# Hybrid trunk step on one core: head order, D's decay and first conv, diagonal taps, norm sums, final store

## The reference

```python
h = rmsnorm(x, norm_pre)
p = split_cols(h @ w_in)
oa = s5_branch(...); ob = hgrn2_branch(...); oc = gla_branch(...)
od = rglru_branch(...)                  # width-4 conv, then RG-LRU; decay = -8 * r * softplus(-lam)
oe = mem_attend(p["e_q"], mk, mv)       # 4 heads over 256 memory tokens, mk, mv from rmsnorm(mem)
pb = einsum("ntcw,cwd->ntcd", branches * silu(gates), w_branch)
merged = einsum("ntcd,ntcd->ntd", sigmoid(h @ w_merge), pb)
x = x + rmsnorm(merged @ w_out, norm_post)
```

## Time and profile before

| | |
|---|---|
| median of 3 runs | 2093.11 us (2087.61 to 2093.49) |
| the profiled execution's own time | 2093.22 us |
| its span, first to last instruction | 2091.4 us |
| TensorE busy | 1990.5 us (95%) |
| DVE, ACT, POOL busy | 61%, 43%, 20% |
| mean granted TensorE clock | 0.974 |

### The profile page before, as it was taken

One profiled execution on the slowest core, in us unless ns is written; L12 is line 12 of the kernel. 1 busy time (PEld: TensorE's weight loads), 2 busy tenths in 40 slices (PEclk: granted clock), 3 DMA queues, 4 the chain that ended last, 5 costly groups with the idle time before them and its releaser, 6 DMA issues.

```text
span 2091.4 us, 36635 instructions
## 1 busy us (share of the span) xinstructions
PE 1990.5 (95%) x15254; PEld 1906.4 (91%) x15254; DVE 1278.6 (61%) x2092; ACT 906.3 (43%) x1307; POOL 411.4 (20%) x708
## 2 busy tenths in 40 slices
PE   6999986999999999999999999999999999999995
PEld 5889986999998989898999999999999999999994
DVE  6654437777665656565777777777565565554543
ACT  4533433444553434343555555545333333433342
POOL 3678877875000000000000000000100000000000
PEclk9999998999998989898999999999999999999997
DMA  6766754555443434444444444444655444555441
GB/s 237 256 245 243 264 181 134 174 182 187 157 159 134 160 136 151 145 149 159 139 143 153 141 150 144 147 140 137 219 165 191 161 155 149 193 178 165 151 162 66
DMA packets 91222, 350.46 MB, mean 168 GB/s; under 512 B 11728, under 2 KB 11872, under 8 KB 87472
## 3 DMA queue, kind: packets, MB, share of 16 engines
q1 hardware_dynamic: 76032, 278.17, 40.3%
q0 software_dynamic: 12144, 49.85, 6.7%
q10 hardware_dynamic: 2880, 20.09, 2.5%
HBM read 321.15 MB, written 26.92 MB: 166 GB/s over the span
## 4 chain that ended last, share of the span: by engine, by line
PE 58%; DVE 7%; ACT 4%; issue 3%; DMA 0%; POOL 0%; ACTq 0%; DVEq 0%
PE ps L1581 57%; DVE w_lo L1034 2%; DVE g_X L1028 1%; DVE g_X L1034 1%; ACT g_t L566 1%; ACT w_hi L566 1%; ACT L566 1%; DVE g_X L1037 0%; ACT g_X L566 0%; DMA a_h<-in_a_h 0%; DVE g_b L1439 0%; PE ps L1869 0%; DVE acc L1031 0%; DVE acc L1028 0%; DVE g_k L1034 0%
## 5 line engine op out<-in xcount | busy, mean ns | idle before, releaser
L1581 PE MATMUL ps<-h_hi,w_hi 128*128 128x288 f32 x2960 | 892.9, 302 | 39.6 <-DVE w_lo L1034 22.9
L1034 DVE TENSOR_TENSOR w_lo<-raw,w_hi 128x1024 fp32r<-128x1024 f32 x522 | 649.6, 1255 | 439.5 <-ACT w_hi L566 436.0
L1581 PE MATMUL ps<-h_hi,w_lo 128*128 128x288 f32 x2960 | 877.8, 297 | 0.0
L1581 PE MATMUL ps<-h_lo,w_hi 128*128 128x288 f32 x2960 | 875.4, 296 | 0.0
L566 ACT ACTIVATE w_hi<-raw 128x1024 fp32r<-128x1024 f32 x522 | 547.3, 1056 | 655.3 <-PE ps L1581 646.9
L1581 PEld LDWEIGHTS ps<-h_hi,w_hi 128*128 128x128 f32 x2960 | 559.7, 189 | 60.6 <-issue 43.0
L1581 PEld LDWEIGHTS ps<-h_hi,w_lo 128*128 128x128 f32 x2960 | 560.7, 189 | 2.3 <-issue 1.9
L1581 PEld LDWEIGHTS ps<-h_lo,w_hi 128*128 128x128 f32 x2960 | 561.7, 190 | 0.0
L1581 PE MATMUL ps<-br_hi,w_hi 128*128 128x288 f32 x640 | 196.0, 306 | 0.5 <-DVE d_gate L1040 0.5
L1581 PE MATMUL ps<-br_hi,w_lo 128*128 128x288 f32 x640 | 192.9, 301 | 0.0
L1581 PE MATMUL ps<-br_lo,w_hi 128*128 128x288 f32 x640 | 192.6, 301 | 0.0
(11 more groups left out here) (369 smaller groups left out, 2465.0 us busy)
## 6 DMA issues: line engine op xcount, KB each, us to landing
raw<-in_w SPq DMA_DIRECT2D x522, 512.0 KB, 3.8
w_scratch<-st_wide POOLq DMA_DIRECT2D x72, 128.0 KB, 3.2
a_w<-w_scratch POOLq DMA_DIRECT2D x8, 1152.0 KB, 7.6
acc<-in_kc ACTq DMA_DIRECT2D x4, 2048.0 KB, 9.3
vc<-in_vc ACTq DMA_DIRECT2D x4, 2048.0 KB, 9.4
c_S<-in_gla POOLq DMA_DIRECT2D x4, 1024.0 KB, 6.1
out_gla_s<-c_S POOLq DMA_DIRECT2D x4, 1024.0 KB, 4.2
h_S<-in_hgrn POOLq DMA_DIRECT2D x8, 512.0 KB, 3.7
```

Of the source, the lines that this page charges most:

```text
L1034: return dve.tensor_tensor(out, a, b, ALU.subtract)
L1581: return pe.matmul(out, a, b, start=start, stop=stop)
```

## The change

Eight edits at once, with no change of what is computed:

1. x's norm: each quarter of squares is summed by two additions (2 x 288, then 288) and not by a reduction over a strided axis. The memory's squares are summed by DVE from 16 to 4 tiles, TensorE adds 4 and not 16, and does it between the two units of `eq 1`.
2. `eq 0`: for each quarter, the matmuls with `h_hi` run once `high` is there; only the four with `h_lo` wait for `split`.
3. E: `ev 2i` before the scores, `fill[0]` before the transposes of `vT`; ACT copies `vm` behind the first query.
4. D's decay in three pieces under heads 0, 1, 2, its columns in `rstd`'s space; conv of tile 0 (`conv(0)`, the old lines 1186 to 1200 as a function) under head 3; DVE's `w_lo` of the next four (two) units ahead of the wait for `e_o`.
5. A: `prepare` makes the raw taps in 128x32 strips, 8 matmuls of 128 columns; `a_K` is 128 x 4 x 32; `outputs` applies them in 32x32 diagonal tiles, 16 matmuls.
6. `out 0` waits for `o_lo` tile by tile.
7. The store of y by SP, in parts of 4, 4, 4, 2, 1, 1 tiles.

```diff
+Y_PARTS = ((0, 4), (4, 4), (8, 4), (12, 2), (14, 1), (15, 1))
...
-        a_K = sb("a_K", [P, 4, P], F32, v_st)
+        a_K = sb("a_K", [P, 4, 32], F32, v_st)
...
+            for n, (k, width) in enumerate(Y_PARTS):
+                sp.wait_ge(S("y_ready"), n + 1)
+                sp.dma_start(t["out_y"][:, k:k + width], acc[:, k:k + width]).then_inc(S("y_stored"), 16)
+            sp.wait_ge(S("y_stored"), 16 * len(Y_PARTS))
...
-                sg(dve.tensor_reduce(gate_t[:, q], sq[:, q * 4:q * 4 + 4].rearrange("p k t -> p t k"), AX.X, ALU.add), "x_ksum")
+                link(add(sq[:, 4 * q:4 * q + 2], sq[:, 4 * q:4 * q + 2], sq[:, 4 * q + 2:4 * q + 4]))
+                sg(add(gate_t[:, q], sq[:, 4 * q], sq[:, 4 * q + 1]), "x_ksum")
...
-            upto(5)
+            for half in range(2):
+                k = 8 * half
+                dve.wait_ge(S("squared"), 5 + half)
+                link(add(sq_m[:, k:k + 4], sq_m[:, k:k + 4], sq_m[:, k + 4:k + 8]))
+                sg(add(sq_m[:, k:k + 2], sq_m[:, k:k + 2], sq_m[:, k + 2:k + 4]), "m_ksum")
+                upto(4 + half)
...
                     upto(END["eg", 2 * i + 3] + 2)
                     gated(2 * i + 3)
+                    decay(i)
+                    upto(END["eg", 2 * i + 3] + 4)
                 else:
                     upto(END["gE", 2])
+                    dve.wait_ge(S("d_params"), 48)
+                    conv(0)
+                    upto(END["gE", 2] + 2)
                 dve.wait_ge(S("e_o"), i + 1)
...
+            def decay(step):
+                lam = d_cols[:, 7]
+                y, z, z2, poly = d_sp[:, 0], d_sp[:, 1], d_sp[:, 3], d_sp[:, 4]
+                if step == 0:
+                    dve.wait_ge(S("d_cols_landed"), 16)
+                    link(ts(d_sp[:, 2], lam, -1.0, 0.0, ALU.mult, ALU.max))
+                    link(ts(d_sp[:, 3], lam, 0.0, None, ALU.max))
+                    sg(add(d_sp[:, 1], d_sp[:, 2], d_sp[:, 3]), "d_abs_lam")
+                    sg(ts(d_sp[:, 5:7], d_cols[:, 5:7], 0.5, None, ALU.mult), "d_halved")
+                elif step == 1:
+                    dve.wait_ge(S("d_exp_lam"), 1)
...
+                    for odd in (13, 11, 9):
+                        link(mul(poly, poly, z2))
+                        link(ts(poly, poly, 1.0 / odd, None, ALU.add))
+                else:
+                    for odd in (7, 5, 3, 1):
+                        link(mul(poly, poly, z2))
+                        link(ts(poly, poly, 1.0 / odd, None, ALU.add))
+                    link(mul(poly, poly, z))
+                    link(stt(poly, poly, 2.0, d_sp[:, 2], ALU.mult, ALU.add))
+                    link(ts(d_sp[:, 7], poly, -LRU_C / 2, None, ALU.mult))
...
             for i in range(4):
+                if i == 1:
+                    act.wait_ge(S("d_abs_lam"), 1)
+                    f(d_sp[:, 0], d_sp[:, 1], ACT.Exp, "d_exp_lam", scale=-1.0)
...
-                raw_taps = ps[:, 7].rearrange("p (n g c) -> p n g c", n=4, g=8)
+                raw_taps = ps[:, 7, 0:P].rearrange("p (n h c) -> p n h c", n=4, h=2)
...
-            project(("eq", 0), h_hi, h_lo, wait_x={0: 1, 4: 2, 8: 3, 12: 4})
-            for k in range(KT):
-                if k % 8 == 0:
-                    pe.wait_ge(S("squared"), 4 + k // 8 + 1)
-                ins = mm(ps[:, 3, 0:N_MEM], ones[:], sq_m[:, k], k == 0, k == KT - 1)
-            sg(ins, "norm_summed")
-            h("eq", 1)
+            for q in range(4):
+                if q % 2 == 0:
+                    pe.wait_ge(lo_ready, q // 2 + 1)
+                pe.wait_ge(S("high"), q + 1)
+                for k in range(4 * q, 4 * q + 4):
+                    mm(out, w_hi[:, k // UK, k % UK], h_hi[:, k], k == 0, False)
+                    mm(out, w_lo[:, k // UK, k % UK], h_hi[:, k], False, False)
+                pe.wait_ge(S("split"), q + 1)
+                for k in range(4 * q, 4 * q + 4):
+                    ins = mm(out, w_hi[:, k // UK, k % UK], h_lo[:, k], False, k == KT - 1)
...
+            def mem_sum():
+                for k in (0, 1, 8, 9):
+                    pe.wait_ge(S("m_ksum"), k // 8 + 1)
+                    ins = mm(ps[:, 3, 0:N_MEM], ones[:], sq_m[:, k], k == 0, k == 9)
+                sg(ins, "norm_summed")
+
+            project(("eq", 1), h_hi, h_lo, between=mem_sum)
...
                 for v in range(2):
                     project(("ek", 2 * i + v), m_hi, m_lo, N_MEM, wait_x={0: 5, 8: 6} if i + v == 0 else ())
+                project(("ev", 2 * i), m_hi, m_lo, N_MEM)
...
-                project(("ev", 2 * i), m_hi, m_lo, N_MEM)
                 project(("ev", 2 * i + 1), m_hi, m_lo, N_MEM)
+                project(fill[0], h_hi, h_lo)
...
                 sg(ins, "e_vt")
-                for n in range(2):
-                    project(fill[n], h_hi, h_lo)
+                project(fill[1], h_hi, h_lo)
...
                 for k in range(2):
-                    ins = mm(ps[:, 7], w[:, 0, k], w[:, 4:8, k], k == 0, k == 1)
+                    for pair in range(4):
+                        own = slice(32 * pair, 32 * pair + 32)
+                        ins = mm(ps[own, 7, 0:P], w[:, 0, k, own], w[:, 4:8, k, own], k == 0, k == 1)
...
-                    mm(y[:, :, n:BLK], a_K[:, n], u[:, :, 0:BLK - n], n == 0, False)
+                    for pair in range(4):
+                        own = slice(32 * pair, 32 * pair + 32)
+                        mm(y[own, :, n:BLK], a_K[own, n], u[own, :, 0:BLK - n], n == 0, False)
...
-            pe.wait_ge(S("o_lo"), KT)
             for n in range(KT):
-                project(("out", n), o_hi, o_lo)
+                project(("out", n), o_hi, o_lo, wait_x={} if n else {k: k + 1 for k in range(KT)}, split="o_lo")
```

More of the change, by code:

```diff
@@ L194, in build @@
         d_st = ExitStack()
[L195 to L196 removed]
+        d_cols = rstd[:, 0:64].rearrange("p (a b) -> p a b", a=8)
+        d_sp = rstd[:, 64:128].rearrange("p (a b) -> p a b", a=8)
         d_cbuf = sb("d_cbuf", [P, WT, NB, 3], F32, d_st)
@@ L265, in build @@
         a_y, a_gs, a_gate = rstd, sd, chunks
+        diagonal = levels[:, 1024:1056]
+        in_pair = levels[:, 1056:1058]
         a_B = levels[:, 0:1024].rearrange("p (n k s) -> p n k s", n=4, k=2)
@@ L553, in _ @@
             load(x_res[:], t["x"], "res_landed")
[L554 to L557, removed]
             pool.wait_ge(S("a_stored"), 16)
-            pool.wait_ge(S("y_stored"), 64)
         @block.scalar
@@ L645, in _ @@
                 f(m_hi[:, ks], mem[:, ks], ACT.Copy, "high")
+            load(d_cols, t["d_cols"], "d_cols_landed")
             half_gate(1)
@@ L699, in _ @@
                         gate("E", v)
+                    if v == 0:
+                        act.wait_ge(S("e_vt"), i + 1)
+                        f(vm[:], ps[:, 6].rearrange("p (a b) -> p a b", a=2), ACT.Copy, "e_vm")
                 act.wait_ge(S("e_pt"), i + 1)
@@ L1125, in _, with conv @@
             sg(dve.reciprocal(st_den, st_den), "a_inverse")
+            def conv(i):
+                wait_taken(dve, "dx", i)
+                link(dve.tensor_copy(d_xs[:, :, 0:3], d_cbuf[:, i]))
+                xp, xs = xc[:, 0:SEQ], by_seq(xc)
+                for j in range(4):
+                    w = d_cols[:, j, i:i + 1]
+                    if j == 0:
+                        bias = d_cols[:, 4, i:i + 1]
+                        link(ts(xp, d_xp[:, 0:SEQ], w, bias, ALU.mult, ALU.add))
+                        link(ts(xs, d_xs[:, :, 0:NT], w, bias, ALU.mult, ALU.add))
+                    else:
+                        link(stt(xp, d_xp[:, j:j + SEQ], w, xp, ALU.mult, ALU.add))
+                        ins = stt(xs, d_xs[:, :, j:j + NT], w, xs, ALU.mult, ALU.add)
+                        link(ins) if j < 3 else sg(ins, "d_xc")
+                link(dve.tensor_copy(d_clast[:, i, 0:1, :], d_xp[:, SEQ:SEQ + 3].unsqueeze(1)))
+                link(dve.tensor_copy(d_clast[:, i, 1:N_SEQ, :], d_xs[:, :, NT:NT + 3]))
@@ L1185, in _ @@
                     upto(END["bE", 2 * i])
[L1186 to L1200, removed]
+                    conv(i)
                 if i:
@@ L1572, in _ @@
             wait_taken(dve, "out", KT - 2)
-            for q in range(4):
-                ks = slice(q * KT // 4, (q + 1) * KT // 4)
-                link(mul(acc[:, ks], acc[:, ks], rstd[:].unsqueeze(1).to_broadcast([P, KT // 4, T])))
+            for k, n in Y_PARTS:
+                ks = slice(k, k + n)
+                link(mul(acc[:, ks], acc[:, ks], rstd[:].unsqueeze(1).to_broadcast([P, n, T])))
                 sg(add(acc[:, ks], acc[:, ks], x_res[:, ks]), "y_ready")
@@ L1602, in project @@
                     sg(ins, units_done)
+                    if u == 0 and between:
+                        between()
             def h(name, n):
```

49 lines of the change are left out of this document (19 added, 30 removed).

## The result

| | median | runs | ratio to before, 95% interval |
|---|---|---|---|
| before | 2092.66 us | 2087.61 to 2093.49 | |
| changed | 2033.95 us | 2030.77 to 2035.41 | 0.9722, 0.9703 to 0.9742 |
| predicted | 2030.9 us | range 2019 to 2047 | |

The account below looks back on a forecast made before the run. TensorE, busy 1990.5 of 2091.4 us, was taken as the bound, except at the two ends. Savings of 8.9 + 10.6 + 21.1 + 8.0 + 0 + 6.4 + 7.3 = 62.3 from 2093.2 gave 2030.9 us, range 2019 to 2047.

Parts of the forecast that it names:

- E: Stage E: waits for `vT` and before the scores go, 12.3 us, less 1.7 of new loss; net 10.6 saved.
- `out`: Before and in `out`: the 4.7 us wait for `o_lo` and 1.7 of half-speed loss go, 6.4 together.
- the end: Kernel's end: SP's smaller last store avoids waiting on POOL's 6.93 us closing DRAIN; 7.3 saved (5.5 to 8).
- The start: Up to `ek 0`: additions 2.4, earlier `eq 0`, fewer memory sums 5.0; 8.9 saved in all (6.5 to 10.5).
- the additions' 2.4: x's norm at the start: additions for the four reductions end 2.6 us earlier, taken as 2.4.
- the new loss, put at 1.7: E: decay on DVE makes `w_lo` of the next head's second `ek` 1.0 and 0.3 late; 1.7 in all (0 to 4).
- D's head: Before D: moving decay and conv removes the 18.9 us wait and 2.2 of slow clock in `dg 0`; 21.1 saved.
- it is paced by `dg 0` and stays: D's first tile: the chain from `d_gates` to the first `d_out` was to be late next but unchanged, at no cost.
- POOL's preparation: POOL's work for A ends at 505.2, its first user comes about 535 (578 less 42.6); 30 us left, no cost.
- the third rival: Work behind E: clock falls at other places, -3 to +12 us, 2028 to 2043; chance 0.08 shared with D's head beyond range.
- A: Stage A: `prepare`'s taps in strips save 1.0 us a tile, eight times, 8.0; diagonal taps in `outputs` gain 0.
- the first rival: A's taps: the four diagonal tiles run one after another, 4.35 us more each, eight times 35: 2066; chance 0.12.

Follow-up runs that it names:

- experiment 7: Changed kernel with start's sums by reductions and y stored in four equal parts: 2035.79 us; separately, with y's six stores issued by GpSimd's queue: 2039.63 us.
- the second profile of the changed kernel: The changed kernel itself run again, unaltered, on the chip of the version with two GpSimd pauses: 2037.31 us, ratio to before 0.9738.
- experiment 1: Part of GpSimd's arithmetic for A (products of `times`, masking in `keep`) left out: changed kernel 2026.88 us, kernel before 2086.45 us.
- experiment 5: Changed kernel with decay and D's first conv put back behind E, all else as changed: 2041.39 us, ratio to before 0.9756.
- experiment 2: Changed kernel with all of GpSimd's arithmetic for A's weights and tables left out, DMAs and a few fills kept: 2022.09 us, ratio to before 0.9667.
- Experiments 2 and 4: 2 has its own line; 4 is the changed kernel with GpSimd paused: short pause 2029.82, long 2033.17, both 2029.47 us, unaltered again 2037.31.
- again: The changed kernel itself run a second time, for comparison with the version with two GpSimd pauses: 2037.31 us, D 260.8 us.
- experiments 6 and 7: 7 has its own line; 6 is the changed kernel with all four of A's taps done on one diagonal tile before the next: 2062.87 us, ratio 0.9876.
- experiment 3: Kernel before with one wait that starts GpSimd's weights 38 us later: 2093.17 us, ratio 1.0010 to before (2090.62).

## Why the prediction was right, and where not

**The total, in part by luck.** The saving came out 3.6 us below the forecast with a miss of 8.8 inside it: E, `out`, the end and C with B paid 6.1 more than was said, and hid most of D's loss.

**The start, right.** 8.9 forecast, 8.7 measured; the additions' 2.4 are shown by experiment 7. Only the inner shares differ: `eq 0` waited 1.2 and 2.3 us for `h_lo`, at two places and not only at the end.

```profile
25.52 0.80 PE L1614 MATMUL ps<-h_lo,w_hi 128*128 128x288 f32 x4 [1.23 <-DVE h_lo L1041]
...
29.64 0.80 PE L1614 MATMUL ps<-h_lo,w_hi 128*128 128x288 f32 x4 [2.26 <-DVE h_lo L1041]
```

**E, right, two terms mis-sized.** The waits went as said. The sum took them at the table's 12.3; from start to start each cost some 0.16 more (a gap of 1783 ns in a delay of 1937 over a matmul's usual spacing), 13.5 in eight. And the new loss, put at 1.7, was one wait of 0.35 us at 176.4, and nothing at all in the second profile of the changed kernel. The piece that was to be 1.0 late is this, DVE in the second head:

```profile
171.05 0.46 DVE L1047 SCALAR_TENSOR_TENSOR gate_t<-half_out,ps 128x288 f32<-128x288 f32 x1 [7.46 <-ACT half_out L569]
...
174.55 3.28 DVE L1041 TENSOR_TENSOR w_lo<-raw,w_hi 128x1024 fp32r<-128x1024 f32 x2
```

It takes 3.1 us here (171.42 to 174.55), not the 4.3 taken from the earlier trace rows. Those rows were stretched by POOL already: in the kernel before without POOL's arithmetic (experiment 1) the stretch with decay and conv is 23.59 us, not 27.80. The two `w_lo` behind it are then stretched (3.28 for 2.4).

**D's head, right for the sum, the reason only in part.** 21.1 forecast, 21.2 measured. But the forecast gave it all to the moved decay and conv; by experiment 5, 11.9 of it stay when these are moved back, since the `w_lo` of `dg 0` now stand ahead of them. `dg 0` and what stands behind it run at full clock:

```profile
286.35:292.93 6.58, 6.58 (x51) 6.58 (x51) 5.77 (x5) 3.94 (x5) 5.79 (x8) 1.00 0.75 246
```

**D's tiles, wrong.** The failed step is the sentence "it is paced by `dg 0` and stays", said of the chain to the first `d_out`, and, for the tiles behind, that no term stood for them at all. That chain had 0.5 to 1.0 us of wait in each tile before, so it was at its limit already; moved by 35 us against POOL's preparation it met more of POOL and lost 8.8. The 8.8 come apart so: TensorE's waits in D went from 7.8 to 15.2 us, 7.4 more, and the fall of the clock at 405.8 costs 1.7, 9.1 together. In the changed kernel's second profile it is 7.6 of waits and three falls (5.1), for 12.1. So the third rival (the clock falls at other places) had a part in D too. These falls came with the longer waits: D shows none in the kernel before, and none in experiment 2. Experiments 2 and 4 show that POOL is the cause: without POOL's arithmetic D is 247.8, with POOL still the first stretch is 19.86. In five profiled executions with the changed kernel's E and D (changed, again, and experiments 6 and 7) D took 256.1 to 260.8, so the 8.8 were no accident, though their places vary: 2.2 to 2.4 in the first stretch each time, 1.6 to 4.8 in the second, some 3 in the fourth in four of the five. The forecast did speak of POOL's preparation, but only of its end. There it has a slip of its own: it takes 42.6 us from 578, where its first three terms make 40.6. And 578 is where `cr 0`'s matmuls begin; ACT first needs the tables behind them, at 549.96 in the changed kernel, 44 us after POOL's end and not 30.

**A, right, the size off.** 0.8 a tile instead of 1.0, 6.5 in eight; the other 0.7 of the 7.2 is a shorter wait ahead of the first tile's taps (0.6 for 1.4), which was not forecast. The 1.88 us of the earlier trace rows reach to the modelled end of the last record; up to the next record the old taps took 1.32. The new ones take 0.57 (16 records, start 1506.57, next matmul 1507.14), not 0.8:

```profile
1506.57 0.65 PE L1614 MATMUL ps<-a_w 128*32 128x128 f32 x16
1507.14 0.40 PE L1614 MATMUL ps<-h_hi,w_hi 128*128 128x288 f32 x1
```

So the strips were better than thought and the old form cheaper. The transposes ahead are 0.1 longer, the first record behind 0.3 shorter, and some 0.1 went at other changes of form: 0.8. The taps stayed at 1.49 for 1.45, as the forecast took it. The rule cited for the first rival (Trainium skill, TensorEngine Tiling (Array Packing), Restrictions and Gotchas) doesn't hold here, for diagonal 32x32 tiles on disjoint partitions of one bank: four run together, 1.49 us against 4.12.

**`out`, right.** 4.8 for the wait (4.7), 2.4 in `out` (1.7). The stretch at 0.50 of the earlier trace rows is gone:

```profile
1912.02:1915.40 3.38, 3.38 (x28) 3.38 (x27) 2.33 (x5) 1.39 (x2) 0.00 (x0) 1.00 0.44 155
```

Seventeen records stood in 3.4 us before, 28 now. Other executions of the same end gave 1.6, so the 0.7 above the forecast is scatter.

**The end, right.** 8.2 for 7.3; the last store, issued at 2030.56, landed 1.7 us later, where 2.6 were taken. (The forecast's own terms, 2081.0, 2.6 and 0.4 against 2091.4, make 7.4.)

**C and B** gave 1.6 by one fall of the clock that was 3.4 us shorter than its like in C's first head. In the second profile it was not. That, like the fall in D, is the third rival, at its smallest.

## What to carry to other kernels

When a change moves stages in time against a long background job of GpSimd, put a term on it: look at which VectorE chains run beside its arithmetic before and after, with the min and the max of one operation as the price. A stage whose chain waits 0.5 to 1 us in each tile is at its limit and takes up any stretching at once. Count what stands behind a longer wait as well: here 3.4 us of half speed followed several of them. And when work is moved off a stall together with the order of what stands before it, undo each of the two alone before giving the gain to either.

## What the hardware showed

- One VectorE operation beside GpSimd's arithmetic can take several times its time: `d_L` 364 and up to 722 ns, `w_lo` 1225 and up to 2709, `d_u` 0.46 and up to 2.07 us. In the stretch up to 560 us these are operations with two operands in SBUF, or a `tensor_scalar` or copy with its one there; with an operand in PSUM (`d_gate`) 455 stays 455. GpSimd's DMAs alone, which experiment 2 kept, left `w_lo` at 1289 at most.
- The same part of GpSimd's work left out (experiment 1) saves 4 us in the kernel before (2090.62 to 2086.45) and 7 in the changed one (2033.95 to 2026.88). Left out wholly (experiment 2) it saves 12 in the changed one; the kernel before was not run so. In experiment 3 the slower executions have the lower granted clock (2104.2 us at 0.970, 2086.6 at 0.976).
- One stretched `d_u` comes back as one wait of TensorE, some 9.5 us later and longer by the same amount: 2.07 and 2.21 us, 2.06 and 2.20, 1.64 and 1.75 (with `d_u` at 0.46 the wait is some 0.6).
- GpSimd's closing DRAIN lasted 6.9 to 7.0 us in the four profiles where GpSimd issued the last store, and 13.5 to 14.8 in the ten where SP issued it and GpSimd's DRAIN began at 1765 to 1803 us; SP's lasted 0.007 to 0.12. What makes it the longer one was not tried.
- Four 32x32 tiles on the diagonal, all writing one PSUM bank, run together.
